# Two per-head norms of an RWKV-7 stage, turned from wide rows to eight numbers per token

## The reference, cut to what matters

```python
    kk = heads(k * k_k).astype(F32)
    kk = kk / jnp.maximum(jnp.sqrt(jnp.sum(kk * kk, axis=-1, keepdims=True)), 1e-12)
...
    def step(state, inp):
        r_t, w_t, k_t, v_t, a_t, b_t = inp
        sa = jnp.einsum('bhvk,bhk->bhv', state, a_t)
        state = state * w_t[:, :, None, :] + sa[..., None] * b_t[:, :, None, :] + v_t[..., None] * k_t[:, :, None, :]
        y = jnp.einsum('bhvk,bhk->bhv', state, r_t)
        return state, y
...
    y = y_f + y_b
    mean = jnp.mean(y, axis=-1, keepdims=True)
    var = jnp.mean(jnp.square(y - mean), axis=-1, keepdims=True)
    yn = ((y - mean) * lax.rsqrt(var + RWKV_GN_EPS)).reshape(b, s, d) * lnx_w.astype(F32) + lnx_b.astype(F32)
    out = (yn + (bonus_f + bonus_b).reshape(b, s, d)) * g.astype(F32)
```

## Time and profile before

| | us |
|---|---|
| median of three runs | 3253.37 |
| the profiled execution, its own time | 3254.34 |
| its span | 3252.6 |
| TensorE busy over the span | 3033.1 (93%) |
| VectorE busy | 1839.9 (57%) |
| ScalarE busy | 1393.7 (43%) |
| GpSimd busy | 669.0 (21%) |
| first y of the tail / last y (L3216) | 2446.2 / 2818.9 |

### The profile page before, as it was taken

One profiled execution on the slowest core, in us unless ns is written; L12 is line 12 of the kernel. 1 busy time (PEld: TensorE's weight loads), 2 busy tenths in 40 slices (PEclk: granted clock), 3 DMA queues, 4 the chain that ended last, 5 costly groups with the idle time before them and its releaser, 6 DMA issues. The chain is left out here.

```text
span 3252.6 us, 59877 instructions
## 1 busy us (share of the span) xinstructions
PE 3033.1 (93%) x25454; PEld 2411.6 (74%) x25454; DVE 1839.9 (57%) x2665; ACT 1393.7 (43%) x2369; POOL 669.0 (21%) x542
## 2 busy tenths in 40 slices
PE   8989999999978999999989999889689989799999
PEld 6757788887746788887658888767577777588887
DVE  6665543445665543446665736474476867457464
ACT  6555422235455422234464424345465655244242
POOL 1000311211000310212001101143275746011010
PEclk9989999999989999999999999989899999799999
DMA  4101333332101323332013323335311111133232
GB/s 148 52 2 65 104 97 94 94 96 82 56 5 62 96 96 97 93 98 78 1 53 92 109 85 101 100 104 194 131 49 30 49 36 45 44 98 109 79 99 83
DMA packets 82344, 260.72 MB, mean 80 GB/s; under 512 B 9632, under 2 KB 13216, under 8 KB 81824
## 3 DMA queue, kind: packets, MB, share of 16 engines
q1 hardware_dynamic: 71424, 235.39, 23.0%
q10 hardware_dynamic: 10656, 21.50, 1.8%
HBM read 235.89 MB, written 20.97 MB: 79 GB/s over the span
## 5 line engine op out<-in xcount | busy, mean ns | idle before, releaser
L1698 DVE TENSOR_TENSOR mlp_w_lo<-mlp_ring,mlp_w_hi 128x1024 fp32r<-128x1024 f32 (+1 forms) x211 | 251.7, 1193 | 573.0 <-ACT mlp_w_hi L1675 572.9
L1675 ACT ACTIVATE mlp_w_hi<-mlp_ring 128x1024 fp32r<-128x1024 f32 (+1 forms) x211 | 213.3, 1011 | 642.2 <-PE ps L1636 637.3
L1698 DVE TENSOR_TENSOR ffn_w_lo<-ffn_ring,ffn_w_hi 128x1024 fp32r<-128x1024 f32 (+3 forms) x172 | 224.2, 1304 | 438.2 <-ACT ffn_w_hi L1675 438.2
L1675 ACT ACTIVATE ffn_w_hi<-ffn_ring 128x1024 fp32r<-128x1024 f32 (+3 forms) x172 | 187.3, 1089 | 480.8 <-PE ps L1636 476.0
L1635 PE MATMUL ps<-mlp_more_parts,mlp_w_hi 128*128 128x512 f32 x952 | 372.3, 391 | 0.0
L1634 PE MATMUL ps<-tiles_parts,mlp_w_hi 128*128 128x512 f32 x832 | 329.7, 396 | 1.1 <-issue 1.1
L1634 PE MATMUL ps<-ffn_x_parts,ffn_w_hi 128*128 128x512 f32 x792 | 312.6, 395 | 18.2 <-DVE ffn_x_parts L2413 14.2
L1636 PE MATMUL ps<-tiles_parts,mlp_w_lo 128*128 128x512 f32 x832 | 327.7, 394 | 0.0
L1634 PE MATMUL ps<-mlp_more_parts,mlp_w_hi 128*128 128x512 f32 x760 | 304.7, 401 | 19.1 <-DVE mlp_w_lo L1698 10.8
L1635 PE MATMUL ps<-ffn_x_parts,ffn_w_hi 128*128 128x512 f32 x792 | 310.3, 392 | 0.0
L1636 PE MATMUL ps<-ffn_x_parts,ffn_w_lo 128*128 128x512 f32 x792 | 310.2, 392 | 0.0
(11 more groups left out here) (504 smaller groups left out, 6188.5 us busy)
## 6 DMA issues: line engine op xcount, KB each, us to landing
ffn_ring<-in_w_ffn_up SPq DMA_DIRECT2D x88, 512.0 KB, 3.6
mlp_ring<-in_w_up SPq DMA_DIRECT2D x64, 512.0 KB, 3.6
mlp_ring<-in_w_down SPq DMA_DIRECT2D x64, 512.0 KB, 3.6
rwkv_keep<-ffn_ring ACTq DMA_DIRECT2D x64, 256.0 KB, 2.5
sq<-rwkv_keep SPq DMA_DIRECT2D x64, 256.0 KB, 3.0
ffn_ring<-in_w_ffn_down SPq DMA_DIRECT2D x16, 768.0 KB, 4.2
in_ring<-in_w_in SPq DMA_DIRECT2D x22, 512.0 KB, 3.6
mlp_ring<-in_w_in SPq DMA_DIRECT2D x22, 512.0 KB, 3.6
```

The source lines that it names most:

```text
L1675: nc.scalar.activation(w.w_hi[:, n % SPLIT, 0:width], w.ring[:, n % RING, 0:width], ACT.Copy).then_inc(s["w_hi_ready"], 1)
L1698: nc.vector.tensor_tensor(w.w_lo[:, n % SPLIT, 0:width], w.ring[:, n % RING, 0:width], w.w_hi[:, n % SPLIT, 0:width].bitcast(F32), ALU.sub ...
```

## The change

Both norms are summed per token. Four products take the squares as the stationary operand, 128 tokens at a time, and stream two columns of ones, so that [128 tokens, 8] sums stand in PSUM (two heads by four token tiles). VectorE adds eps or floors, and takes the reciprocal of 128x8 numbers; ScalarE takes the square root of these, reading each 64 times over, so that a 128x512 row of scales by token comes out; four TensorE transposes turn it back to channels, and VectorE multiplies straight from PSUM. The mean of y is gone: V's transpose against the identity becomes a product with a centring matrix (identity minus 1/64 inside each head). The scans move from beats 22 and 24 to 30 and 34, the scaled y from 38 to 21, the key's product from 33 to 22, the square of y from 20 to 4, the two roots from 25 and 22 to 19 and 20, and four GpSimd steps by one to three beats. The masks' table grows by 128 columns.

```diff
...
+    row, to = np.arange(P)[:, None], np.arange(P)[None, :]
+    r[:, RMASKS["centre"]:RMASKS["centre"] + P] = (row == to) - (row // HD == to // HD) / HD
...
+        norms = sb("norms", [P, 2, 2 * NT])
...
+        OF_Y, OF_K = range(2)
+        centre = masks[:, RMASKS["centre"]:RMASKS["centre"] + P]
...
+        def per_head(which):
+            return norms[:, which, :].unsqueeze(2).broadcast_to([P, 2 * NT, HD])
...
-                        mm = nc.tensor.transpose(m.ps[:, n % 2, kind * P:(kind + 1) * P], src[:, tile_at(t)], m.ident)
+                        into = m.ps[:, n % 2, kind * P:(kind + 1) * P]
+                        if kind == KIND_V:
+                            if n == 0:
+                                pe.wait_ge(s["masks_in"], 16)
+                            nc.tensor.matmul(into, src[:, tile_at(t)], centre, start=True, stop=True)
+                        else:
+                            mm = nc.tensor.transpose(into, src[:, tile_at(t)], m.ident)
...
-                def mean_sums(c, main):
-                    pe.wait_ge(s["y_ready"], c + 1)
+                def head_sums(bank, squares):
+                    for t in range(NT):
+                        mm = nc.tensor.matmul(m.ps[:, bank, 2 * t:2 * t + 2], squares[:, tile_at(t)], m.head_ones[:, ::HD], start=True, stop=True,
+                                              skip_group_check=True)
+                    return mm
+                def spread_back(bank, wide):
+                    for t in range(NT):
+                        mm = nc.tensor.transpose(m.ps[:, bank, tile_at(t)], wide[:, tile_at(t)], m.ident)
+                    return mm
+                def var_sums(c, main):
+                    pe.wait_ge(s["squared"], c + 1)
...
-                    nc.tensor.matmul(m.ps[:, 0, :], m.head_ones, y[:], start=True, stop=True).then_inc(s["y_sums"], 1)
+                    head_sums(0, rs).then_inc(s["var_sums"], 1)
+                def var_spread(c):
+                    pe.wait_ge(s["tail_root"], c + 1)
+                    spread_back(0, rs).then_inc(s["tail_spread"], 1)
...
-                    nc.tensor.matmul(m.ps[:, 1, :], m.head_ones, t8[:, KK, :], start=True, stop=True).then_inc(s["kk_sums"], 1)
+                    head_sums(1, t8[:, KK, :]).then_inc(s["kk_sums"], 1)
+                def kk_spread(c):
+                    pe.wait_ge(s["root_ready"], c + 1)
+                    spread_back(1, t8[:, KK, :]).then_inc(s["kk_spread"], 1)
...
-                def var_sums(c):
-                    pe.wait_ge(s["squared"], c + 1)
-                    nc.tensor.matmul(m.ps[:, 0, :], m.head_ones, rs[:], start=True, stop=True).then_inc(s["var_sums"], 1)
...
-                            pe.wait_ge(s["tail_root"], c - 1)
+                            pe.wait_ge(s["scaled"], c - 1)
...
-                            pe.wait_ge(s["root_ready"], c + 2)
+                            pe.wait_ge(s["kk_ready"], c + 2)
...
-                        mean_sums(i - 2, main)
+                        var_sums(i - 2, main)
...
+                        if pair == 0 and oldest:
+                            var_spread(i - 2)
+                    if new:
+                        kk_spread(i + 1)
...
-                    if oldest:
-                        var_sums(i - 2)
...
-                    if k == 20:
-                        act.wait_ge(s["centred"], c + 1)
+                    if k == 4:
+                        act.wait_ge(s["y_ready"], c + 1)
...
-                    if k == 25:
-                        act.wait_ge(s["var_sums"], c + 1)
-                        nc.scalar.activation(rs[:], m.ps[:, 0, :], ACT.Sqrt, scale=1.0 / HD, bias=gn_eps[:, 0:1]).then_inc(s["tail_root"], 1)
+                    if k == 19:
+                        act.wait_ge(s["tail_inverse"], c + 1)
+                        nc.scalar.activation(rs[:].rearrange("p (i n) -> p i n", i=2 * NT), per_head(OF_Y), ACT.Sqrt).then_inc(s["tail_root"], 1)
...
-                    if k == 22:
-                        act.wait_ge(s["kk_sums"], c + 1)
-                        nc.scalar.activation(t8[:, KK, :], m.ps[:, 1, :], ACT.Sqrt).then_inc(s["root_ready"], 1)
+                    if k == 20:
+                        act.wait_ge(s["inverted"], c + 1)
+                        nc.scalar.activation(t8[:, KK, :].rearrange("p (i n) -> p i n", i=2 * NT), per_head(OF_K), ACT.Sqrt).then_inc(s["root_ready"], 1)
...
-                    if k in (30, 33):
-                        d = (k - 30) // 3
+                    if k in (32, 36):
+                        d = (k - 32) // 4
...
-                    if k in (36, 38):
-                        d = (k - 36) // 2
+                    if k in (37, 38):
+                        d = k - 37
...
                     if k == 19:
-                        dve.wait_ge(s["y_sums"], c + 1)
-                        nc.vector.scalar_tensor_tensor(out=y[:], in0=m.ps[:, 0, :], scalar=-1.0 / HD, in1=y[:], op0=ALU.mult, op1=ALU.add).then_inc(s["centred"], 1)
-                    if k in (30, 34):
-                        dve.wait_ge(s["tail_root"], c + 1)
-                        part = slice((k - 30) * S // 8, (k - 26) * S // 8)
-                        nc.vector.reciprocal(rs[:, part], rs[:, part]).then_inc(s["tail_inverse"], 1)
-                    if k == 38:
-                        dve.wait_ge(s["tail_inverse"], 2 * c + 2)
-                        nc.vector.scalar_tensor_tensor(out=y[:], in0=y[:], scalar=param("ln_w", c), in1=rs[:], op0=ALU.mult, op1=ALU.mult).then_inc(s["scaled"], 1)
+                        dve.wait_ge(s["var_sums"], c + 1)
+                        nc.vector.tensor_scalar(norms[:, OF_Y, :], m.ps[:, 0, 0:2 * NT], 1.0 / HD, GN_EPS, ALU.mult, ALU.add).then_inc(s["var_ready"], 1)
+                        dve.wait_ge(s["var_ready"], c + 1)
+                        nc.vector.reciprocal(norms[:, OF_Y, :], norms[:, OF_Y, :]).then_inc(s["tail_inverse"], 1)
+                    if k == 21:
+                        dve.wait_ge(s["tail_spread"], c + 1)
+                        nc.vector.scalar_tensor_tensor(out=y[:], in0=y[:], scalar=param("ln_w", c), in1=m.ps[:, 0, :], op0=ALU.mult, op1=ALU.mult).then_inc(s["scaled"], 1)
...
-                    if k in (22, 24):
-                        d = (k - 22) // 2
+                    if k in (30, 34):
+                        d = (k - 30) // 4
...
-                    if k == 25:
-                        dve.wait_ge(s["root_ready"], c + 1)
-                        nc.vector.tensor_scalar(t8[:, KK, :], t8[:, KK, :], 1e-12, None, ALU.max).then_inc(s["floored"], 1)
-                    if k in (28, 31):
+                    if k == 19:
+                        dve.wait_ge(s["kk_sums"], c + 1)
+                        nc.vector.tensor_scalar(norms[:, OF_K, :], m.ps[:, 1, 0:2 * NT], 1e-24, None, ALU.max).then_inc(s["floored"], 1)
...
-                        part = slice((k - 28) * S // 6, (k - 25) * S // 6)
-                        nc.vector.reciprocal(t8[:, KK, part], t8[:, KK, part]).then_inc(s["inverted"], 1)
-                    if k == 33:
-                        dve.wait_ge(s["inverted"], 2 * c + 2)
-                        nc.vector.tensor_tensor(t8[:, KK, :], t8[:, KK, :], t8[:, KR, :], ALU.mult).then_inc(s["kk_ready"], 1)
+                        nc.vector.reciprocal(norms[:, OF_K, :], norms[:, OF_K, :]).then_inc(s["inverted"], 1)
+                    if k == 22:
+                        dve.wait_ge(s["kk_spread"], c + 1)
+                        nc.vector.tensor_tensor(t8[:, KK, :], m.ps[:, 1, :], t8[:, KR, :], ALU.mult).then_inc(s["kk_ready"], 1)
...
```

17 lines of the change are left out of this document (8 added, 9 removed).

## The result

| | kernel before | changed kernel |
|---|---|---|
| median of 13 runs | 3250.59 us (3244.02 to 3257.19) | 3259.61 us (3254.38 to 3265.02) |
| profiled execution, its own time | 3254.34 us | 3262.44 us |
| its span | 3252.6 us | 3260.6 us |

The ratio is 1.0028, 95% interval 1.0019 to 1.0038: slower by 9 us (6 to 12), where I had forecast +1.5 and "same", meaning within 0.2%. The time lies in my range of 3249 to 3260, but by luck. That range was set around a median of three runs, 3253.37; over thirteen runs the kernel before has 3250.59. Taken as differences my range was -4 to +7, and +9 lies outside it. The profiled executions differ by about the same amount (8.0 in the span), so they can be compared term by term.

What follows compares the result with a forecast made beforehand. TensorE, busy 93% of the span, was taken as the bound, with MERGE limited by both VectorE and ScalarE. The terms 7.2 + 2.0 - 2.4 + 1.5 - 2.5 - 4.3 = +1.5 gave 3255 us, range 3249 to 3260.

Steps and rivals of the forecast that it cites:

- the centring: FRONT: V's product takes two records instead of one, 0.11 more per turn; +7.2 us over eight iterations, bounds +6 to +14.
- The rival of a switch on each side: FRONT: a product between transposes costs a switch on each side; +7 beyond the forecast, 3262 us; chance 0.08.
- the narrow sums and the small operations: Eight records of narrow sums about 0.9 us together; VectorE's two operations on 128x8 0.17 each.
- the new chain: MIDDLE: TensorE would not wait for sums, root and spread, with 0.3 us in hand at the tightest.
- the term of MIDDLE: MIDDLE gains 0.2 per tail (six) and loses 0.45 per key (seven): +2.0 us, bounds -1 to +5.
- another pattern of half-clock stretches: Anything else, such as TensorE's half-clock stretches lying differently; no size given, chance 0.05.
- MERGE: The 1.48 us gap stays, also limited by ScalarE; small waits go, about 0.3 per iteration: -2.4 us, bounds 0 to -12.
- VectorE was the bound: MERGE: the 1.48 and 0.5 us more go in six iterations, 12 instead of 2.4; 3245 us; chance 0.2.
- The GpSimd rival: MERGE: GpSimd's decay work, waiting for the later scans, becomes the bound; +8 us, 3263; chance 0.12.
- iteration -1: Nothing hides there; the scans start 3.9 us later and A at 2341.2: +1.5 us, bounds 0 and +3.9.
- iteration 8: Only scan and tail: mean's product gone -1.1, reciprocals' delays gone -1.4; together -2.5 us (-1 to -3.5).
- the last tail: Iteration 9, without company: 7.8 us becomes 3.5, so -4.3 us (-3.8 to -4.8).

Runs made afterwards that it cites:

- e8: The changed kernel with two unused products of 128x256 in TensorE's wait ahead of the first narrow sums: 3258.25 us, +8.8 against the kernel before.
- e5: The kernel before with the centring alone, no mean product, both norms on 128x512 as they were: 3250.06 us, +2.9 against the kernel before.
- e1: The changed kernel with one unused 128x512 product added right ahead of each of the two groups of narrow sums: 3265.33 us, +13.7 against the kernel before.
- e10: The kernel before with the centring and the narrow norm of the head outputs, key's norm and scans as before: 3251.58 us, +2.3 against the kernel before.
- e2: The changed kernel with the key's narrow sums moved behind the first half of the value products: 3267.70 us, +14.0 against the kernel before.
- e3: The changed kernel with one small unused exponential on ScalarE ahead of MERGE, taking the table load out of it: 3265.36 us, +11.4 against the kernel before.
- e9: The changed kernel with the small exponential ahead of MERGE, scans and GpSimd's steps at old beats, and two unused 128x256 products in TensorE's wait: 3257.59 us, +7.5.
- e4: The kernel before with one small unused exponential on ScalarE ahead of MERGE: 3250.44 us, 0.0 against the kernel before.
- e6: The changed kernel with VectorE's two scans and GpSimd's steps behind them at their old beats: 3267.87 us, +16.3 against the kernel before.

## Why the prediction was right and wrong

**Right: the centring.** Every turn costs 0.11 more and there is no switch cost; +5.9 for +7.2 (FRONT alone +5.1, a little under my lower bound of +6; the rest is in SUMMED). The rival of a switch on each side fell with the row spacing, and the centring alone measures +2.9 with the mean's product gone.

**Right: the narrow sums and the small operations as single items**, 0.88 us for eight records from start to start, 0.17 and 0.20 on VectorE, no wait for the new chain. The eight MIDDLEs at full clock, with the lengths that e8 shows for the same instructions (4.32, 5.25, five times 6.80, 5.52), are 49.1 us: +1.1, for my +2.0.

**Wrong: the term of MIDDLE as a whole.** I had "MIDDLE gains 0.93 - 0.74 = 0.2 per tail and loses 0.45 per key: +2.0 in all, bounds -1 to +5". It was +15.0 in the profile. The 13.9 beyond the full-clock length are TensorE at its lower level. The failed step is "the two sums that stay cost TensorE what they did: 0": true of their own time, untrue of what they do to the clock of what follows. I priced records at the clock of the row they came from, and kept "another pattern of half-clock stretches" in a rest of 0.05. The rows show it: of five full MIDDLEs none is slowed without narrow groups (the kernel before, e5) or with wide products added beside them (e1), one with one narrow group (e10), and five, five or three with two (the changed kernel, e2, e3). Each is one execution.

**How much of the +9 is the clock?** Less than the 13.9 of MIDDLE suggest. Stretches that were in MERGE and iteration 8 before are in MIDDLE now, and some of their cost went with them. The granted clock of every execution is on record. Its mean is 0.9726 over the 88 of the kernel before that ran beside the experiments (0.9725 to 0.9727 in each of the four series) and 0.9708 over the 13 of the changed kernel. From these, an estimate: the lower level lasts 178 us before and 190 after, 12 us more. Were all of it on the path it would cost 6 us. Among the 88, an execution with one microsecond more of it is 0.30 us longer (correlation 0.77), and by that it would cost 3.5. Neither figure counts that a stretch may cost more in MIDDLE than where it lay before. So 3 to 6 of the 9 us come out as the net change of the clock. The rest, 3 to 6 us, is other work and waits, where my sum had +1.5. The same means warn against giving the clock the whole: in e8 and e9, which carry added products but mostly in waits, it is 0.9729, as good as in the kernel before, and they are still +8.8 and +7.5. How the nine microseconds divide is not shown beyond this.

**MERGE: right about the limit, right in size by luck.** The sum is -3.9 for -2.4, but I had about -0.3 in each iteration, behind tail work. In the five full iterations MERGE grew by some 1 us in all (131.1 to 132.0), although the kernel before had three stretches at the lower level there and the changed kernel none; the -3.9 comes from iterations 0, 1 and 7 (-1.5, -1.1, -2.3). ScalarE's load was the second limit (e3 against e4), so VectorE's 4 us bought nothing in the full ones. The rival "VectorE was the bound" is out. The GpSimd rival did not happen in the changed kernel (2.5 us of waits for NM), but it was next in line: with ScalarE out of the way it took 12.3 us.

**Too small: iteration -1**, +2.8 for +1.5. My bounds (0 to 3.9) held it. Moving the scans back gives 2.0 of it. I had let A start at 2341.2, and it did (2341.16). What I had left out is that the two BK products behind A take 3.41 us for 2.35 before. GpSimd's products now lie beside them. That part is not the late scans': in e6 they take 3.41 as well.

```profile
2334.92 2.33 DVE L3292 TENSOR_TENSOR_SCAN x<-heads_restart,sq 128x512 f32<-128x512 f32 x2
2341.16 3.04 DVE L3308 SCALAR_TENSOR_TENSOR heads_A<-x 128x512 f32<-128x512 f32 x2 [3.90 <-ACT x L3079]
2344.12 3.41 DVE L3315 TENSOR_TENSOR heads_BK<-x,heads_EN 128x512 f32<-128x512 f32 x2
```

**Too small: iteration 8**, -4.9 for -2.5, beyond my bound. The lower level lasted 14.1 us here instead of 26.1, which my term did not have. **Right: the last tail**, -4.6 for -4.3:

```profile
2832.71 1.05 PE L2795 MATMUL ps<-c,rstd 128*128 128x2 f32 x8 [2.10 <-ACT rstd L3051]
2834.92 1.02 PE L2801 MATMUL ps<-c,rstd 128*128 128x128 f32 x4 [1.16 <-ACT rstd L3054]
```

## What to carry to other kernels

A TensorE product is not priced by its own time alone. Here several in a row were made narrow, behind a wait, and the clock of what followed went to its lower level. Look at the granted clock of the stretch behind the edit, first where TensorE is the bound, and then at its mean over the whole execution, for a stretch in one place may be one less in another. Before an engine is relieved at a wait, ask who else is late there, and try it by taking that one away in both kernels: here ScalarE stood behind VectorE, and GpSimd behind ScalarE. And a stretch freed of a loss in one profile is no gain until the medians show it.

## What the runs showed of the hardware

- TensorE's clock fell while TensorE was busy: 8.39 of MIDDLE's 8.40 us, with 0.78 us of waiting ahead of it. The Trainium skill's "TensorE: Matmul & The Clock Gate", section "Why this matters for your kernels", names idle gaps between bursts as what to keep away; that alone does not describe this place, where the wait was as long before the change (0.83) with the clock at 1.00.
- The stretches at the lower level lie elsewhere after small edits: in FRONT (e9) or MERGE (e1) instead of MIDDLE, and in MIDDLE instead of MERGE and iteration 8 in the changed kernel. In the MERGEs of e1 that hold one, it is 26.1 to 27.7 us long against the changed kernel's 26.15; in MIDDLE one costs 1.6 (8.37 against 6.80).
- A VectorE operation with two SBUF inputs took 0.74 us where GpSimd was idle and up to 5.84 beside GpSimd's steps (e6).
- "issue" as a releaser ahead of a product can hide a real wait: the 1.65 us vanished with ScalarE's table load.
